# Two feed-forwards on one Trainium2 core: three 256-column products per weight block against one of 512 columns and one of 256

## What is computed

```python
# first block, FFN_HIDDEN = 2816
ff = einsum('bsf,fd->bsd', silu(einsum('bsd,df->bsf', h2, w_gate)) * einsum('bsd,df->bsf', h2, w_up), w_down)
# second block, D_FF = 4096
...relu(einsum('bsd,df->bsf', xn, w_ff1)) ** 2 @ w_ff2
```

## Time and profile before

| | |
|---|---|
| median of 3 runs | 876.49 us (876.12 to 876.52) |
| profiled execution | 875.93 us, span 874.1 us |
| TensorE busy | 863.9 us, 6680 products |
| VectorE busy | 583.5 us |
| ScalarE busy | 445.1 us |
| weight transfers | 129 of 1 MB, median 5.0 us from issue to landing |

### The profile page before, as it was taken

The page is one execution under the profiler, slowest core; times in us unless marked ns, Lnnn a source line. Parts: engine busy times, 40 slices in busy tenths (PEclk is TensorE's granted clock), DMA queues, the critical chain, the costliest instruction groups (busy, mean ns, idle before and its releaser), DMA issues.

```text
span 874.1 us, 15188 instructions
## 1 busy us (share of the span) xinstructions
PE 863.9 (99%) x6680; PEld 832.1 (95%) x6680; DVE 583.5 (67%) x705; ACT 445.1 (51%) x519; POOL 93.9 (11%) x71
## 2 busy tenths in 40 slices
PE   9999999999999999999999999999999999999998
PEld 8999999999999899999999899998998999999998
DVE  6967994775767586556555687787777755555454
ACT  7578764554444374344343464476566644344441
POOL 1002550551000000000000001000441000000000
PEclk9999999999999999999999999999999999999999
DMA  8645343442455445555555546544221555555551
GB/s 326 244 153 186 121 140 125 145 142 100 137 172 186 190 148 193 193 192 180 175 184 187 191 148 200 191 150 145 97 98 49 169 175 187 193 187 174 174 189 49
DMA packets 21266, 143.92 MB, mean 165 GB/s; under 512 B 2594, under 2 KB 2610, under 8 KB 4688
## 3 DMA queue, kind: packets, MB, share of 16 engines
q1 hardware_dynamic: 20016, 139.47, 46.8%
q0 software_dynamic: 1040, 3.43, 1.2%
q10 hardware_dynamic: 144, 0.04, 0.0%
HBM read 141.87 MB, written 1.06 MB: 164 GB/s over the span
## 4 chain that ended last, share of the span: by engine, by line
PE 86%; DVE 7%; ACT 4%; DMA 1%; issue 1%; SPq 0%; POOL 0%; DVEq 0%
PE ps L1549 22%; PE ps L1550 21%; PE ps L1551 21%; PE ps L1713 3%; PE ps L1800 2%; PE ps L1799 2%; PE ps L1801 2%; DVE wlo L850 2%; ACT whi L428 1%; PE ps L1615 1%; PE ps L1621 1%; PE ps L1618 1%; DMA x<-xT 1%; ACT work L732 1%; PE ps L1804 1%
## 5 line engine op out<-in xcount | busy, mean ns | idle before, releaser
L1549 PE MATMUL ps<-xh,whi 128*128 128x256 f32 x1656 | 475.0, 287 | 1.7 <-DVE wlo L850 1.4
L1550 PE MATMUL ps<-xl,whi 128*128 128x256 f32 x1656 | 468.5, 283 | 0.0
L1551 PE MATMUL ps<-xh,wlo 128*128 128x256 f32 x1656 | 468.4, 283 | 0.0
L850 DVE TENSOR_TENSOR wlo<-raw,whi 128x2048 fp32r<-128x2048 f32 x129 | 297.4, 2308 | 135.5 <-ACT whi L428 134.8
L428 ACT ACTIVATE whi<-raw 128x2048 fp32r<-128x2048 f32 x129 | 246.2, 1912 | 160.0 <-DMA raw<-w 159.5
L1549 PEld LDWEIGHTS ps<-xh,whi 128*128 128x128 f32 x1656 | 317.5, 192 | 5.3 <-issue 2.7
L1550 PEld LDWEIGHTS ps<-xl,whi 128*128 128x128 f32 x1656 | 317.6, 192 | 0.5
L1551 PEld LDWEIGHTS ps<-xh,wlo 128*128 128x128 f32 x1656 | 317.4, 192 | 0.0
L357 POOL TENSOR_TENSOR work<-work 128x512 f32<-128x512 f32 x28 | 57.3, 2067 | 119.0 <-DVE work L1004 52.8
L631 ACT ACTIVATE xh<-work 128x512 fp32r<-128x512 f32 x27 | 17.1, 633 | 82.0 <-DVE work L1512 41.2
L909 DVE TENSOR_TENSOR work<-ps,bcs 128x512 f32<-128x512 f32 x34 | 23.4, 688 | 20.2 <-PE ps L1551 18.4
(11 more groups left out here) (267 smaller groups left out, 938.0 us busy)
## 6 DMA issues: line engine op xcount, KB each, us to landing
raw<-w SPq DMA_DIRECT2D x129, 1024.0 KB, 5.0
raw<-w SPq DMA_DIRECT2D x4, 512.0 KB, 8.0
x<-xT SPq DMA_DIRECT2D x2, 512.0 KB, 6.2
work<-bias_scratch POOLq DMA_DIRECT2D x1, 1024.0 KB, 9.3
out<-x SPq DMA_DIRECT2D x4, 256.0 KB, 2.3
work<-lnr POOLq DMA_DIRECT2D x1, 512.0 KB, 4.0
work<-sgw POOLq DMA_DIRECT2D x1, 512.0 KB, 4.7
lvl_s<-lvl POOLq DMA_DIRECT2D x1, 448.0 KB, 4.3
```

The source lines that it names most:

```text
L850: V.tensor_tensor(wlo[:, slot, :], raw[:, slot, :], whi[:, slot, :].bitcast(F32), ALU.subtract)\
L1549: mm(out, hi, xh[:, tile, :], start=start, stop=False, skip_group_check=skip)
L1550: mm(out, hi, xl[:, tile, :], start=False, stop=False, skip_group_check=skip)
L1551: return mm(out, wlo[:, slot, at:at + width], xh[:, tile, :], start=False, stop=stop, skip_group_check=skip)
```

## The change

It applies to FFN1 pairs 2 to 10 (gate and up, 18 units) and FFN2 pairs 1 to 13 and 15 (14 units), 32 units of 16 blocks. `xh` and `xl` become two halves of one tile `xx`, so that the high and the low part of a tile of x are 512 neighbouring columns. Per block TensorE issues one product of `whi` with all 512 columns and one of `wlo` with the 256 high ones, into the first half of the bank. An output tile then has a bank to itself, its sum in two halves: ScalarE copies the second half out (`low_copy`), VectorE adds the first half to it (`low_added`). A gate uses banks 0 and 1, an up 2 and 7; FFN2 alternates between these two pairs. Pair 1 of FFN1 and pairs 0 and 14 of FFN2 stay as they were, but for their banks.

```diff
-        xh = sb("xh", [P, 20, T], F32R)
-        xl = sb("xl", [P, 20, T], F32R)
+        xx = sb("xx", [P, 20, 2, T], F32R)
+        xh, xl = xx[:, :, 0, :], xx[:, :, 1, :]
...
+            def low_copy(u, m, dst):
+                n, banks = WIDE[u]
+                if m == 0:
+                    act.wait_ge(sem("wide_tile"), n + 1)
+                else:
+                    filled(u)
+                A(dst[:, m, :], ps[banks[m]][:, T:2 * T], ACT.Copy).then_inc(sem("low_copy"), 1)
...
             for j in range(1, PAIRS1):
                 u = U_F1 + 3 * j - 1
+                wide = j in WIDE1
+                if wide:
+                    low_copy(u, 0, lows[0])
                 split_hi(u + RING)
+                if wide:
+                    low_copy(u, 1, lows[0])
+                    low_copy(u + 1, 0, lows[1])
                 silu_pair(j)
                 if j < PAIRS1 - 1:
                     split_hi(u + 1 + RING)
+                if wide:
+                    low_copy(u + 1, 1, lows[1])
                 hidden_hi(j, "hid", 2 * (j % 2), j % 2)
...
+            def low_added(u, m, out, low):
+                n, banks = WIDE[u]
+                dve.wait_ge(sem("low_copy"), 2 * n + m + 1)
+                return V.tensor_tensor(out[:, m, :], ps[banks[m]][:, 0:T], low[:, m, :], ALU.add)
+            def gate_wide(j, u):
+                dve.wait_ge(sem("gated"), j)
+                count(low_added(u, 0, two(silu), lows[0]))
+                link(low_added(u, 1, two(silu), lows[0]))
+                V.tensor_tensor(two(silu), two(silu), factors_by_tile(2), ALU.mult).then_inc(sem("gate_r"), 1)
...
+            def square_wide(j, u, slot_h):
+                dve.wait_ge(sem("hid2_y"), j)
+                count(low_added(u, 0, two(silu), lows[j % 2]))
+                link(low_added(u, 1, two(silu), lows[j % 2]))
+                dve.wait_ge(sem("hid2_lo"), j)
+                V.scalar_tensor_tensor(hid[slot_h], two(silu), 0.0, two(silu), ALU.max, ALU.mult).then_inc(sem("hid2_y"), 1)
...
+            def wide_tiles(u, base):
+                for m in range(2):
+                    o = ps[WIDE[u][1][m]]
+                    for k in range(8):
+                        w = slice((8 * m + k) * P, (8 * m + k + 1) * P)
+                        mm(o[:, :], whi[:, u % SLOTS, w], xx[:, base + k, :, :], start=k == 0, stop=False)
+                        last = mm(o[:, 0:T], wlo[:, u % SLOTS, w], xh[:, base + k, :], start=False, stop=k == 7)
+                    if m == 0:
+                        last.then_inc(sem("wide_tile"), 1)
+                return last
...
             def ffn1_step(j, u):
                 first = j == 1
                 pe.wait_ge(sem("lo_ready"), u + 1)
-                if not first:
+                if j in WIDE1:
                     pe.wait_ge(sem("gate_r"), j)
-                used(pair_tiles(u, 8, between=(lambda: norm_bc("n3")) if first else None))
+                    pe.wait_ge(sem("hid_y"), j)
+                    used(wide_tiles(u, 8))
...
             def ffn2_step(j, u):
                 pe.wait_ge(sem("lo_ready"), u + 1)
-                used(pair_tiles(u, 0))
+                if j in WIDE2:
+                    if j > 1:
+                        pe.wait_ge(sem("hid2_y"), j - 1)
+                    used(wide_tiles(u, 0))
```

More of the change, by code:

```diff
@@ L54 @@
 KEYS_BANK = (U_UQ + 2) % RING
+WIDE1 = range(2, PAIRS1)
+WIDE2 = [j for j in range(1, PAIRS2) if j != PAIRS2 - 2]
+GATE_BANKS, UP_BANKS = (0, 1), (2, 7)
 PAR = {}
@@ L137, with wide_units @@
 TURNED = dict(mo=(1, 2, 0, 7), ff=(3, 4, 7, 0))
+def wide_units():
+    units = []
+    for j in WIDE1:
+        units += [(U_F1 + 3 * j - 1, GATE_BANKS), (U_F1 + 3 * j, UP_BANKS)]
+    for j in WIDE2:
+        units.append((U_F2 + 2 * j - 1, (UP_BANKS, GATE_BANKS)[j % 2]))
+    return {u: (i, banks) for i, (u, banks) in enumerate(units)}
+WIDE = wide_units()
 def z_index(u):
@@ L278, in build_blocks @@
         gated = work[:, 32 * T:34 * T]
+        lows = [view(34, 2), view(36, 2)]
         sgate = view(74, 4, 512)
@@ L815, in relu_pair @@
                 act.wait_ge(sem("unit_used"), u + 1)
-                if not isinstance(j, int) or j >= 1:
+                if j >= 1:
                     act.wait_ge(sem("hid2_y"), j)
@@ L824, in _ @@
                 u = U_F2 + 2 * j - 1
-                ahead(u)
-                relu_pair(j, u, u % RING)
+                if j in WIDE2:
+                    low_copy(u, 0, lows[j % 2])
+                    ahead(u)
+                    low_copy(u, 1, lows[j % 2])
+                else:
+                    ahead(u)
+                    relu_pair(j, u, UP_BANKS[0])
                 hidden_hi(j, "hid2", 8 + 2 * (j % 3), j % 3)
@@ L1180, in hidden, with up_wide, hidden_wide @@
                 V.tensor_tensor(hid[slot_h], two(gated), two(ps[bank][:, :]), ALU.mult).then_inc(sem("hid_y"), 1)
+            def low_added(u, m, out, low):
[7 more added lines that the diff above has]
+                V.tensor_tensor(two(silu), two(silu), factors_by_tile(2), ALU.mult).then_inc(sem("gate_r"), 1)
+            def up_wide(j, u, m):
+                if m == 0:
+                    dve.wait_ge(sem("silu"), j + 1)
+                    dve.wait_ge(sem("hid_y"), j)
+                    V.tensor_tensor(two(gated), two(silu), factors_by_tile(2), ALU.mult).then_inc(sem("gated"), 1)
+                count(low_added(u, m, lows[1], lows[1]))
+            def hidden_wide(j, slot_h):
+                dve.wait_ge(sem("gated"), j + 1)
+                dve.wait_ge(sem("dve_chain"), chained[0])
+                dve.wait_ge(sem("hid_lo"), j)
+                V.tensor_tensor(hid[slot_h], two(gated), lows[1], ALU.mult).then_inc(sem("hid_y"), 1)
             def hidden_lo(j, slot_h, hidden_name, base):
@@ L1196, in _ @@
                 u = U_F1 + 3 * j - 1
-                gate_scaled(j, u, u % RING)
+                wide = j in WIDE1
+                if wide:
+                    gate_wide(j, u)
+                else:
+                    gate_scaled(j, u, u % RING)
                 split_lo(u + RING)
+                if wide:
+                    up_wide(j, u + 1, 0)
                 if j < PAIRS1 - 1:
                     split_lo(u + 1 + RING)
-                hidden(j, j % 2, u + 1, (u + 1) % RING)
+                if wide:
+                    up_wide(j, u + 1, 1)
+                    hidden_wide(j, j % 2)
+                else:
+                    hidden(j, j % 2, u + 1, (u + 1) % RING)
                 hidden_lo(j, j % 2, "hid", 0)
@@ L1508, in relu_square @@
             def relu_square(j, slot_h, slot):
-                dve.wait_ge(sem("relu"), j + 1)
-                if not isinstance(j, int) or j >= 1:
+                dve.wait_ge(sem("relu"), 1 if j == 0 else 2)
+                if j >= 1:
                     dve.wait_ge(sem("hid2_lo"), j)
@@ L1521, in _ @@
                 u0 = U_F2 + 2 * j - 1
-                ahead(u0)
-                relu_square(j, j % 3, u0 % RING)
+                if j in WIDE2:
+                    square_wide(j, u0, j % 3)
+                    ahead(u0)
+                else:
+                    ahead(u0)
+                    relu_square(j, j % 3, UP_BANKS[0])
                 hidden_lo(j, j % 3, "hid2", 8)
@@ L1881, in down, with pair_tiles @@
                 return last
-            def pair_tiles(u, base, between=None):
+            def pair_tiles(u, base, between=None, bank=None):
+                bank = u % RING if bank is None else bank
                 for m in range(2):
@@ L1887, in pair_tiles @@
                     for k in range(8):
-                        last = mm3(ps[u % RING][:, m * T:(m + 1) * T], u % SLOTS, (8 * m + k) * P, base + k, k == 0, k == 7)
+                        last = mm3(ps[bank][:, m * T:(m + 1) * T], u % SLOTS, (8 * m + k) * P, base + k, k == 0, k == 7)
+                return last
[6 more added lines that the diff above has]
+                        last = mm(o[:, 0:T], wlo[:, u % SLOTS, w], xh[:, base + k, :], start=False, stop=k == 7)
+                    if m == 0:
+                        last.then_inc(sem("wide_tile"), 1)
                 return last
@@ L1897, in ffn1_step @@
                 pe.wait_ge(sem("lo_ready"), u + 1)
-                if not first:
+                if j in WIDE1:
                     pe.wait_ge(sem("gate_r"), j)
-                used(pair_tiles(u, 8, between=(lambda: norm_bc("n3")) if first else None))
+                    pe.wait_ge(sem("hid_y"), j)
+                    used(wide_tiles(u, 8))
+                else:
+                    used(pair_tiles(u, 8, between=lambda: norm_bc("n3")))
                 pe.wait_ge(sem("lo_ready"), u + 2)
-                if first:
+                if j in WIDE1:
+                    used(wide_tiles(u + 1, 8))
+                else:
                     pe.wait_ge(sem("gate_r"), 1)
-                else:
-                    pe.wait_ge(sem("hid_y"), j)
-                used(pair_tiles(u + 1, 8))
```

(9 more changed lines are left out.)

## The result

The changed kernel takes 871.94 us (median of 5 runs, 871.83 to 872.31) against 876.49 us, a ratio of 0.995 with a 95% interval of 0.9939 to 0.9961. Predicted were 871.2 us.

The account below looks back on a forecast made before the run. TensorE was taken to bound the kernel, paying the distance between product starts. From 875.93 us, 6.4 for fewer products came off and 1.1 for one stall went on: 870.6 profiled, 871.2 median, range 867.5 to 874.5.

Parts of the forecast that it names:

- TensorE bounds, the price is the distance between starts, and 0.0125 us of it is a product's own: Both feed-forwards: TensorE waits for nearly nobody; each product costs 0.0125 us whatever its width.
- the forecast term: Wide units: 512 blocks save 0.0125 us each, 6.4 us in all, 3.6 in FFN1 and 2.8 in FFN2.
- The pair: Each block of a wide unit: one 512 and one 256 product take 0.3475 us instead of 0.360 for three.
- The stall: FFN1 gates, now waiting for hid_y: 0.54 us left; one late transfer costs 1.1 us, ends none and 3.4 us.
- The sum: Whole kernel: 870.6 us for the profiled execution, the median 0.56 above it, so 871.2 us.
- ScalarE, VectorE, the layout at zero: Wide units: extra copies (24 us), additions (27 us) and the strided xx hide behind TensorE, costing zero.
- FFN2's moved waits: FFN2: the moved work adds less than 2 us to a slack of 5.6 us, costing zero.
- The transfer decides every gate: Rival, FFN1: all nine transfers late, each step stalls about 1.14 us, 10.3 in all, giving 880.4 us; chance 0.05.
- The cheap narrow product: Rival, wide units: the pair costs 0.34 us and no stall falls, 10.2 us go, giving 866.3 us; chance 0.08.

Follow-up runs that it names:

- the kernel with 16 in a row: Changed kernel with the hid_y wait back at the up unit and a unit's 16 wide products before its 16 narrow ones: 869.58 us, ratio 0.9924.
- grouped kernels: Changed kernel with 2, 4, 8 or 16 products of one width in a row, the last two with hid_y wait at up: 869.99, 871.2, 870.03, 869.58 us.
- the grouped kernel: Changed kernel with each output tile's 8 wide products first and its 8 narrow ones behind them: 871.71 us, ratio 0.9949.
- the two other kernels with the same FFN1: Changed kernel with FFN2's wide units all in banks 0 and 1: 872.04 us; changed kernel with wide products in FFN1 alone: 875.42 us.
- the split kernel: Changed kernel with each product of 512 columns issued as two of 256 into the bank's halves: 876.91 us, ratio 1.0003.
- the late kernel: Changed kernel with line 1244's factor and the up's first-tile addition moved behind VectorE's second split_lo, making hid_y later: 875.32 us, ratio 0.9987.
- two in a row: Changed kernel with two wide products, then two narrow ones, four times an output tile: 869.99 us, ratio 0.993.
- the second layout kernel: Kernel before with only xh and xl made halves of one tile, FFN2's units in banks 0, 1, 2 in turn: 877.02 us, ratio 1.0005.

## Why the prediction was right

- **TensorE bounds, the price is the distance between starts, and 0.0125 us of it is a product's own.** Right. The split of the wide product undoes the whole gain; long runs of one width cost 0.227 and 0.120 us, and in the kernel with 16 in a row the two feed-forwards gained 3.7 + 2.7 = 6.4 us, the forecast term. The fixed part of 2.5 ns that the Trainium skill gives ("TensorE: Matmul & The Clock Gate", "Back-to-back issue gap") would by an estimate from it have made 1.3 us of it; the measurements, 4.55 us, and 5.4 to 7.0 us in the grouped kernels without a stall, decide against it.
- **The pair.** The step that failed. "I take the averages of the two long runs, since the odd distances at a change of width are partly rounding and have both signs" set aside the one place of the trace that showed the new situation. The 0.23 and 0.24 behind a narrow product were real, and in strict alternation every wide product is behind a narrow one; the 0.22 ahead of one was rounding (0.226). The pair costs 0.353 us in 25 of 32 units and 0.347 in the others. With the down units of FFN1, longer by 0.036 us each, the term was mis-sized as 6.4 us where 3.9 came.
- **The stall.** Mechanism and chain were right, and the room nearly: 0.54 us by the rows, 0.37 to 0.86 in the trace after from the end of the multiplication to the gate, two stalls in the grouped kernel, and 3.4 us when the room was used up on purpose. Of these distances 0.15 us can't be used, since that much lies between the multiplication and a gate that waits for it; the prediction had it at nothing. The count was one, and none fell in the profiled execution of the changed kernel. Of the two other kernels with the same FFN1, one had a stall (0.2 us net) and one had none. Whether a late transfer hits differs between executions of one program, so a stall here has no certain size; a range was the right answer, a number was luck.
- **The sum.** For the profiled execution 870.6 us were forecast and 871.86 came: the gain of the products 2.5 us short, the stall 1.1 us too many, and 0.2 gained at the end of FFN1. The median then lay only 0.08 us above the profiled execution and not 0.56, so that the sum missed it by 0.7 us. Luck brought it that near.
- **ScalarE, VectorE, the layout at zero.** Right each: the split kernel has all of them and, less its one stall, takes the time of before. FFN2's moved waits cost nothing either: in the changed kernel its one wait is the 1.0 us that the kernel before has too.
- **The rivals.** "The transfer decides every gate" did not come; the late kernel shows that two operations more behind the split make every gate wait, with most transfers on time. The cheap narrow product was half true: 0.11 us behind a wide one, paid back by the wide one behind it.

## What to carry to other kernels

Where TensorE is full, count products as well as columns: here each cost about 0.013 us beside its columns (2 x 0.120 - 0.227), and 512 fewer were worth 4.6 us. Then keep products of one width together: two in a row alone gave 1.9 us more, and 16 in a row, with the wait back at the up unit, 2.4. When a wait is moved ahead, read from the trace how long its chain takes from the transfer on, and put on the waited engine nothing between that chain's last link and the signal; half a microsecond of room is spent by one late transfer.

## What the runs showed that I had not expected

- Right behind narrow products five wide ones in a row are slow: 233, 236, 228, 233 and 231 ns (grouped kernel), then 226 and 227; two narrow ones behind wide ones are quick, 113 and 119, then 120. The round trip costs 0.02 us net (units of 5.567 and 5.587 us with one and two of them).
- In strict alternation the distances repeat every three pairs (241, 120, 236, 113, 233, 117 ns) or settle at 230 and 117, and the same unit with the same operands has one or the other in turn through FFN2. Neither bank nor slot decides it.
- A transfer of 1 MB beside which one packet of instructions is fetched took over 5.44 us in 44 of 208 cases, up to 7.7, and none of 566 did without one. Kernels with the same FFN1 had it at the same place on time in one execution (4.9 us) and late in the other (7.0 us), and executions of one program differ by up to 1.4 us (the second layout kernel, 876.13 to 877.50). One profile shows one of these cases, not the typical one.
